# A hybrid encoder layer on one core: the skip product moved into the gate panel, and the first inputs of three stages loaded a stage earlier

## The reference

```python
h = rms_norm(x, norm1_w)
proj = h @ w_in                      # q, k, v, z, xbc, dt_raw, mq
attn_out = windowed_gqa(rope(norm(q)), rope(norm(k)), v, attn_sink)
ssm_out  = ssd_bidirectional(z, xbc, dt_raw, ...)
mem_out  = memory_attention(norm(mq), norm(mk), mv)
x = x + concat([attn_out, ssm_out, mem_out]) @ w_out
return x + (silu(gate) * up) @ w_ffn_down    # gate, up: conv(rms_norm(x) @ w_ffn_up)

# inside ssd_bidirectional
y_f = ssd_scan(xs, dt[0], ...)               # forward scan
y_b = ssd_scan(reversed xs, dt[1], ...)      # backward scan
y = y_f + y_b + d_skip[:, None] * xs         # the skip product
y = rms_norm(y * silu(z)) * norm_w
```

## Time and profile before

| | us |
|---|---|
| median of 3 runs | 2181.43 |
| profiled execution: device time | 2188.39 |
| profiled execution: span | 2186.6 |
| norm and transpose, first load of projections | 0 to 53 |
| `projections` (gate panel from about 449) | 53 to 531.9 |
| `ssm_forward` | 531.9 to 673.9 |
| `attention` | 673.9 to 918.9 |
| `memory` | 918.9 to 1007.4 |
| `out_projection` | 1007.4 to 1246 |
| `ffn` | 1246 to 2186.6 |

### The profile page before, as it was taken

The page is one execution under the profiler, slowest core; times in us unless marked ns, Lnnn a source line. Parts: engine busy times, 40 slices in busy tenths (PEclk is TensorE's granted clock), DMA queues, the critical chain, the costliest instruction groups (busy, mean ns, idle before and its releaser), DMA issues. The chain is left out here.

```text
span 2186.6 us, 29798 instructions
## 1 busy us (share of the span) xinstructions
PE 2034.9 (93%) x10642; PEld 1737.2 (79%) x10642; DVE 1364.8 (62%) x1936; ACT 607.6 (28%) x1172; POOL 233.3 (11%) x242
## 2 busy tenths in 40 slices
PE   4999999997875999788999799999999999999997
PEld 3887888886764999777888588888888888888885
DVE  6664686533873888683324537757766766766766
ACT  5111122112763666541002221211211111121120
POOL 2000584510341001000000000000000000000000
PEclk8999999999776999999999899999999999999998
DMA  5324223223533111244211121111011121010102
GB/s 174 106 87 121 82 102 105 100 93 136 169 125 126 45 39 49 90 162 184 77 39 43 51 72 29 39 48 29 29 58 29 29 58 29 29 58 29 29 10 96
DMA packets 111122, 164.12 MB, mean 75 GB/s; under 512 B 8736, under 2 KB 68160, under 8 KB 109760
## 3 DMA queue, kind: packets, MB, share of 16 engines
q1 hardware_dynamic: 81792, 119.64, 17.2%
q10 hardware_dynamic: 29248, 43.41, 5.6%
HBM read 125.45 MB, written 37.57 MB: 75 GB/s over the span
## 5 line engine op out<-in xcount | busy, mean ns | idle before, releaser
L2373 PE MATMUL ff_proj<-h_hi,ff_uhi 128*128 128x512 f32 (+1 forms) x1056 | 374.8, 355 | 10.7 <-DVE ff_ulo L2286 10.7
L2373 PE MATMUL ff_proj<-h_lo,ff_uhi 128*128 128x512 f32 (+1 forms) x1056 | 374.7, 355 | 0.0
L2373 PE MATMUL ff_proj<-h_hi,ff_ulo 128*128 128x512 f32 (+1 forms) x1056 | 374.4, 355 | 0.0
L2332 DVE TENSOR_TENSOR x<-x,ff_proj 128x512 f32<-128x512 f32 x264 | 181.5, 688 | 185.3 <-PE ff_proj L2393 183.0
L2373 PEld LDWEIGHTS ff_proj<-h_hi,ff_uhi 128*128 128x128 f32 x1056 | 200.3, 190 | 39.9 <-DVE ff_ulo L2286 11.1
L2373 PEld LDWEIGHTS ff_proj<-h_lo,ff_uhi 128*128 128x128 f32 x1056 | 200.3, 190 | 28.6
L2373 PEld LDWEIGHTS ff_proj<-h_hi,ff_ulo 128*128 128x128 f32 x1056 | 200.1, 190 | 28.0
L638 PE MATMUL pj_bank<-pj_whi,act_hi 128*128 128x512 f32 x400 | 160.3, 401 | 0.0
L638 PE MATMUL pj_bank<-pj_whi,act_lo 128*128 128x512 f32 x400 | 156.5, 391 | 0.0
L638 PE MATMUL pj_bank<-pj_wlo,act_hi 128*128 128x512 f32 x400 | 156.5, 391 | 0.0
L2244 ACT ACTIVATE ff_padded<-ff_proj 128x1024 f32<-128x1024 f32 x44 | 45.2, 1028 | 349.4 <-PE ff_proj L2373 349.4
(11 more groups left out here) (269 smaller groups left out, 4205.6 us busy)
## 6 DMA issues: line engine op xcount, KB each, us to landing
ff_rawu<-w_up SPq DMA_DIRECT2D x44, 512.0 KB, 4.8
pj_raw<-w_in SPq DMA_DIRECT2D x28, 512.0 KB, 3.6
ff_rawd<-w_down SPq DMA_DIRECT2D x22, 512.0 KB, 3.5
sf_rows<-scratch_acs_rows SPq DMA_DIRECT2D x10, 1024.0 KB, 7.5
wo_raw<-w_out SPq DMA_DIRECT2D x16, 512.0 KB, 3.6
scratch_proj<-hd_pieces ACTq DMA_DIRECT2D x30, 256.0 KB, 2.1
n_x<-tokens SPq DMA_DIRECT2D x14, 512.0 KB, 4.3
sf_xc<-scratch_xbc_tiles SPq DMA_DIRECT2D x10, 512.0 KB, 4.1
```

The lines of the kernel that those rows point to most:

```text
L2332: nc.vector.tensor_tensor(v, v, ring(g), ALU.add).then_inc(added, 1)
L2373: m = nc.tensor.matmul(proj[:, g, t0:t0 + n], U[w][:, s, k, g], X[x][:, k, t0:t0 + n], start=(k == 0 and r == 0), stop=(k == KC - 1 and r ...
```

## The change

1. The skip product. `scan_back` gets two operations: `y_back = x_ps * D` (read from PSUM, where x has just been turned), then, once y of the state is multiplied into `scaled`, `y_back = y_back + scaled`. `ssm_forward` loses two: the product into `y2` (L1818) and y2 + y_back (L1829); it adds `y_back` itself to y. The wait of ScalarE's B copy for VectorE's y2 goes too.
2. First inputs of the forward scan (identity, norm weights, x, B, C of tiles 0 and 1) are loaded at the end of SyncE's list in `projections`, into free pieces beside `y_back`. The rows and z of tiles 0 and 1 stay where they were.
3. Inputs of `attention` (all keys as one load, the values, queries of tiles 0 and 1, mask, sink, identity) are loaded at the end of SyncE's list in `ssm_forward`.
4. Inputs of `memory` (identity, keys, values, queries of tiles 0 and 1) are loaded at the end of SyncE's list in `attention`.

In each case SyncE waits for these loads before its block ends, and the waits for them in the next stage are gone.

```diff
@@ projections
-        turn_ident = raw[:, 1, 1, 0:P]
+        turn_ident, skip = raw[:, 1, 1, 0:P], raw[:, 1, 1, P:P + NS]
             sp.dma_start(turn_ident, ident_dram).then_inc(S["const"], 16)
+            sp.dma_start(skip, small["ssm_D"].broadcast_to([P, NS])).then_inc(S["const"], 16)
...
                 sp.dma_start(xc[i % 2], xbc_c[NT - 1 - i]).then_inc(xc_loaded[i % 2], 16)
+            sp.wait_ge(head_done, preps)
+            early = ((R["xc"][:, 0], xbc_c[0]), (R["xc"][:, 1], xbc_c[1]), (R["turn_ident"], ident_dram),
+                     (R["norm_w"], small["ssm_norm_w"].broadcast_to([P, NS * PS])))
+            for dst, src in early:
+                sp.dma_start(dst, src).then_inc(forward_loaded, 16)
+            sp.wait_ge(forward_loaded, 16 * len(early))
@@ scan_back
                 v.tensor_tensor(x_dec, x_ps, factor(dec, t), ALU.mult).then_inc(S["x"], 1)
-                dve.wait_ge(S["off"], i + 1)
+                if i == 0:
+                    dve.wait_ge(S["const"], 32)
...
-                v.tensor_tensor(y_back[:, t].rearrange("p (h q) -> p h q", q=PS), y_ps, factor(e_acs, t),
-                                ALU.mult).then_inc(S["y"], 1)
+                v.tensor_tensor(yb, x_ps, bc(skip.unsqueeze(2), [P, NS, PS]), ALU.mult).then_inc(S["x"], 1)
+                dve.wait_ge(S["off"], i + 1)
+                if i > 0:
+                    dve.wait_ge(S["h"], 2 * i)
+                v.tensor_tensor(scaled, y_ps, factor(e_acs, t), ALU.mult).then_inc(S["y"], 1)
+                dve.wait_ge(S["x"], 2 * i + 2)
+                dve.wait_ge(S["y"], 2 * i + 1)
+                v.tensor_tensor(yb, yb, scaled, ALU.add).then_inc(S["y"], 1)
+                dve.wait_ge(S["y"], 2 * i + 2)
                 v.tensor_tensor(scaled, state, factor(e_tot, t), ALU.mult).then_inc(S["h"], 1)
@@ back_inputs, back_states (TensorE)
-                    pe.wait_ge(S["const"], 16)
+                    pe.wait_ge(S["const"], 32)
-                    pe.wait_ge(S["x"], i)
+                    pe.wait_ge(S["x"], 2 * i)
-                pe.wait_ge(S["x"], i + 1)
+                pe.wait_ge(S["x"], 2 * i + 1)
@@ ssm_forward
-            for dst, src in ((ident[:, :], ident_dram), (wn[:, :], small["ssm_norm_w"].broadcast_to([P, XW])),
-                             (dsk[:, :], small["ssm_D"].broadcast_to([P, NS]))):
-                sp.dma_start(dst, src).then_inc(S["const"], 16)
...
             order(sp, load)
+            ahead.load(sp, proj, k_twice, ident_dram, mask_dram, small["attn_sink"], early_loaded)
...
-            pe.wait_ge(S["const"], 48)
...
-                    act.wait_ge(S["y"], 4 * t - 2)
...
-                v.tensor_tensor(hp(y2[:, :]), x_tok[:, :, :], bc(dsk[:, :].unsqueeze(2), [P, NS, PS]),
-                                ALU.mult).then_inc(S["y"], 1)
...
-                v.tensor_tensor(y2[:, :], y2[:, :], yb, ALU.add).then_inc(S["y"], 1)
...
-                v.tensor_tensor(y[:, s], y[:, s], y2[:, :], ALU.add).then_inc(S["y"], 1)
+                v.tensor_tensor(y[:, s], y[:, s], yb, ALU.add).then_inc(S["y"], 1)
@@ attention: its inputs, loaded in ssm_forward
+    def load(self, sp, proj, k_twice, ident_dram, mask_dram, sink, done):
+        for dst, src in ((self.ident[:, :], ident_dram), (self.sink[:, :], sink.broadcast_to([P, HQ])),
+                         (self.k_two[:, :].rearrange("p t h a d -> p t (h a d)"), keys),
+                         (self.q_raw[:, :].rearrange("p t h d -> p t (h d)"), rows[:, 0:2, 0:1024]),
+                         (self.mask[:, :], mask_dram[1]), (self.v[:, :, :], rows[:, :, 1280:1536])):
+            sp.dma_start(dst, src).then_inc(done, 16)
+        sp.wait_ge(done, 16 * self.LOADS)
...
             tile_loop(sp, load)
+            mem_early.load(sp, mem_proj, proj, ident_dram, memory_loaded)
...
-            pe.wait_ge(S["const"], 16 * 2)
             for t in range(NT):
-                pe.wait_ge(k_loaded[sum(t >= t0 for t0, _ in KEY_PARTS[1:])], 16)
@@ memory
-            pe.wait_ge(S["const"], 16)
             for k in range(NMT):
-                pe.wait_ge(k_loaded[k // MT], 16)
```

More of the change, by code:

```diff
@@ L887, in _, with __init__ @@
             act.wait_ge(row_stored, 32 * NCH)
-def attention(nc, proj, k_twice, ident_dram, mask_dram, small, mix_t):
-    sink = small["attn_sink"]
+class AttentionInputs:
+    LOADS = 6
+    def __init__(self, nc, ctx):
+        b = Bufs(nc, ctx)
+        self.ident = b.sb("at_ident", [P, P])
+        self.mask = b.sb("at_mask", [P, 3 * P])
+        self.sink = b.sb("at_sink", [P, HQ])
+        self.k_two = b.sb("at_ktwo", [P, NT, HKV, 2, DH])
+        self.v = b.sb("at_v", [P, NT, HKV * DH])
+        self.q_raw = b.sb("at_qraw", [P, 2, HQ, DH])
+    def load(self, sp, proj, k_twice, ident_dram, mask_dram, sink, done):
+        rows = proj.rearrange("(t p) n -> p t n", p=P)
+        keys = k_twice.rearrange("(t p) n -> p t n", p=P)
+        for dst, src in ((self.ident[:, :], ident_dram), (self.sink[:, :], sink.broadcast_to([P, HQ])),
[4 more added lines that the diff above has]
+        sp.wait_ge(done, 16 * self.LOADS)
@@ new lines, with __init__, far, load @@
+class MemoryInputs:
+    LOADS = 4
+    def __init__(self, nc, ctx):
+        def far(name, shape):
+            return ctx.enter_context(nc.sbuf_tensor(name, shape, FP32, side="right"))
+        self.ident = far("me_ident", [P, P])
+        self.k_n = far("me_kn", [P, NMT, HM, DM])
+        self.v = far("me_v", [P, NMT, HM, DM])
+        self.q_n = far("me_qn", [P, 2, HM, DM])
+    def load(self, sp, mem_proj, proj, ident_dram, done):
+        kv = mem_proj.rearrange("(t p) n -> p t n", p=P)
+        queries = proj.rearrange("(t p) n -> p t n", p=P)
+        for dst, src in ((self.ident[:, :], ident_dram),
+                         (self.k_n[:, :].rearrange("p t h d -> p t (h d)"), kv[:, :, 0:512]),
+                         (self.q_n[:, :].rearrange("p t h d -> p t (h d)"), queries[:, 0:2, 2048:2560]),
+                         (self.v[:, :].rearrange("p t h d -> p t (h d)"), kv[:, :, 512:1024])):
+            sp.dma_start(dst, src).then_inc(done, 16)
+        sp.wait_ge(done, 16 * self.LOADS)
@@ L901, in attention @@
+def attention(nc, proj, early, mem_proj, mem_early, ident_dram, mix_t):
     WIN = 3 * P
-    KEY_PARTS = ((0, 2), (2, 4), (6, NT - 6))
     with ExitStack() as ctx:
         b = Bufs(nc, ctx)
-        ident = b.sb("at_ident", [P, P])
-        mask = b.sb("at_mask", [P, WIN])
-        k_two = b.sb("at_ktwo", [P, NT, HKV, 2, DH])
-        v_sb = b.sb("at_v", [P, NT, HKV * DH])
+        ident, mask, k_two, v_sb, sinkb, q_raw = early.ident, early.mask, early.k_two, early.v, early.sink, early.q_raw
@@ L1012, in high @@
         def high(act, t, s):
-            act.wait_ge(q_loaded[s], q_loaded_value(t, s))
+            if not (isinstance(t, int) and t < 2):
+                act.wait_ge(q_loaded[s], q_loaded_value(t, s))
             if not (isinstance(t, int) and t == 0):
@@ L1225, in _, with memory @@
                 o_unit(NT - 1, c, units_before(NT - 1) + 3 + c)
-def memory(nc, proj, mem_proj, ident_dram, mix_t, w_out, first):
+def memory(nc, proj, early, mix_t, w_out, first):
     MT = NMT // 2
@@ L1514, in _, with ssm_forward @@
             o_t(NT - 1)
[L1517 removed]
+def ssm_forward(nc, proj, xbc_c, acs_rows, ident_dram, small, R, mix_t, k_twice, mask_dram, ahead):
     XW = NS * PS
@@ L1640, in body @@
                 first = before(t, 1)
-                pe.wait_ge(loaded[s], loaded_value(t, s))
+                if not before(t, 2):
+                    pe.wait_ge(loaded[s], loaded_value(t, s) - 16)
                 if not first:
```

96 lines of the change are left out of this document (33 added, 63 removed).

## The result

The changed kernel takes 2165.24 us, the median of 4 runs (2158.49 to 2167.82), beside 2184.47 us for 4 runs of the kernel before (2181.31 to 2187.79). The ratio is 0.991 (0.9894 to 0.9927): 19.2 us by the medians. A second set of 5 runs gave 2163.05 us and 0.9885 (0.9864 to 0.9906). The profiled execution has a span of 2164.3 us and a time of 2166.04; the sum had put them at 2164.4 and 2166.2. So the size is right in total, and two of the sum's four terms, looked at one by one, are not: the starts of the scan and of the memory stage.

The account below looks back on a forecast made before the run. The prediction took the kernel to be bound by serial stages whose starts wait for loads. Gains of 2.9 (scan), 13.9 (attention), 5.4 (memory) and 0 (skip product) sum to 22.2 us: from 2181.43 to 2159.2 us, range 2149 to 2171.

Parts of the forecast that it names:

- the sum's four terms: Gains at the starts of scan, attention and memory plus the skip product: 2.9 + 13.9 + 5.4 + 0 = 22.2 us.
- Bound by serial starts: Seven blocks run without overlap, so time at a block's start in which nothing computes is kernel time.
- Start of the scan: Forward scan: TensorE starts at once, but the rows are late next, landing in 5.95 us; gain 2.9 us.
- my signs of being wrong: Scan products with other than five 6.9 us runs; VectorE's last panel wait gone; a block's end following a load.
- Start of attention: Attention: TensorE starts at about 673.96 instead of 687.87, the chain of keys keeping its pace; gain 13.9 us.
- Start of the memory stage: Memory stage: TensorE no longer waits for the identity; gain 5.4 us, lower end 1.9.
- rival of the clock: Scan: the alternation of fast and slow tiles shifts; 16.3 us either way; better by over 6 us 0.09, worse 0.10.
- Skip product, 0: Scan: two VectorE operations fewer per tile, hidden by other waits; gain 0, upper end 3.3 us.
- Panel: Gate panel: VectorE's two added operations, 1.4 us per tile, fit its 2.34 us wait; cost 0. Slower rival: 0.02.
- early loads: End of the scan: attention's 5128 KB of loads end some 10 us before the block does and cost nothing.
- spill: End of the scan: rival that prefetch at half rate ends the block 7.5 us later, gain 14.7; chance 0.04.
- all fast: Scan: the clock rival's better case, all ten tiles' products fast, 16.3 us more gain, 2142.9 us.

Follow-up runs that it names:

- e2: The changed kernel with the memory stage's first inputs loaded inside the memory stage again; 2169.86 us, ratio 0.9922.
- e3: The changed kernel with attention's first inputs loaded inside attention again; 2177.77 us, ratio 0.9961.
- e4: The changed kernel with the scan's identity, norm weights and first x, B, C loaded inside the scan again; 2169.67 us, ratio 0.9926.
- f0: The changed kernel run once more, nothing altered; 2163.05 us.
- g3: The kernel before the change with the same unread matmuls at the same places as g1; 2170.22 us, ratio 0.9926.
- g1: The changed kernel with unread matmuls in TensorE's idle stretches in the scan, attention and the memory stage's end; 2142.27 us, ratio 0.9797.
- e1: The kernel before with only the skip product moved to the gate panel; 2185.78 us, ratio 1.0005.
- f1: The changed kernel with three unread matmuls of 384 columns at the end of TensorE's list in attention; 2160.59 us, ratio 0.9897.
- f2: The changed kernel with 28 unread matmuls where TensorE waits in the forward scan; 2149.16 us, ratio 0.9838.
- f3: The changed kernel with the scan's first tile's rows loaded as two transfers; 2160.43 us, ratio 0.9891.
- h1: g1 with the skip product made in the forward scan again, as before the change; 2143.54 us, ratio 0.9810.
- g2: g1 with the first tile's rows also loaded in two transfers; 2145.09 us, ratio 0.9813.

## Why the prediction was right, and where it was not

**Bound by serial starts.** Right. Each of e2, e3 and e4 lengthens its own stage, and by the medians their parts, 21.6 us, are as large as the whole change (19.2 and 21.9).

**Start of the scan, 2.9 us.** The step was right and its size was not: 4.3. I took the rows' landing as 5.95 us, the middle of a load that was alone (5.1) and one in a row of others (6.8); it was 4.6, and 4.5 to 5.0 in the other profiles. The scan gained 5.8 in the profile and 5.1 against e4. What goes beyond 4.3 lies in the tail: from the second product to the last 95.06 us instead of 96.00, and 0.6 us less behind it, with products of 5.81 and 6.43 us where before stood 3.68 and 7.06. That is how the clock fell in this run, the rival that I had named, at a tenth of its price; in f0, the same kernel, the stretch from the second product to the last took 93.67. So one of my signs of being wrong did come: not five slow products but six, three of them at 6.9 us or more and three between the levels.

**Start of attention, 13.9 us.** Right: 13.9 for e3 against after and 13.6 for before against f0, each pair with the same kind of first tile, and 13.7 for g3 against g1. The chain of keys kept its pace too, as I had said: from TensorE's start to the turn of the queries it took 8.42 us, and 8.76 before. That the profiled stage gained only 12.1 is the clock, at 0.51 from 677 to 687 over the first tile's scores. It was low there in e1 and e3 as well, where the loads are late, and not in f0: chance between runs, which the sum had at nothing in this stage.

**Start of the memory stage, 5.4 us.** Wrong in size: 2.8. The step that failed is taking the whole wait as gain. The wait of 5.4 us went, and 2.6 came back, since TensorE came to the first tile at the lower level and stayed there for 12.5 us instead of 3.0. f1 shows that it is the clock: at 0.99 the stage takes 79.48 us, which is 9.0 less than before. I had asked of each start what would be late next among buffers and transfers, and not at what clock the freed engine would work; my rival of the clock was for the scan alone. f0, e3 and e4 repeat it (12 us at the lower level). f2 and f3, with 3 to 4 us of it, show that it doesn't have to be so, and what decides stays open.

**Skip product, 0.** Right: e1 holds 0. h1 adds that the move shows 1.5 to 1.8 us when the slow products are gone; that these hide it otherwise is argued and not shown.

**Panel, early loads, spill.** Right. VectorE's last wait fell by 1.25 us and the tiles kept their 7.9; the loads were down 8 us before the end (I had said some 10).

**The sum.** 22.2 us against 22.3 of the two profiled spans is partly luck: +1.4 from the scan, +1.5 from its tail, +1.4 from chance ahead of it, -1.8 (attention) and -2.6 (memory) from the clock. Against the medians, 19.2 and 21.9, it is 3.0 and 0.3 us high. The forecast of 2159.2 stood 6.0 under the median after, since I took the gain from the median of three runs; over 23 runs the kernel before took 2185.55.

**The rival of the clock** came nearest to mattering. I had priced "all fast" at 16.3 us and given it to chance. It can be brought about: f2 has nine of ten products fast and its scan is 12.0 us shorter. The Trainium skill, "TensorE: Matmul & The Clock Gate", section "HAM oscillation", says that waits between bursts of matmuls throw the clock back each time. The traces agree with it in part: with the waits filled nine of ten products are fast (f2), but unfilled only every second one was slow before, not each.

## What to carry to other kernels

Where stages don't overlap, the time from a stage's first issue to its first work can be summed over the stages, and loads a stage earlier take it away where all the inputs move; here they landed 8 us before that stage's end and cost it nothing. In the scan, where the rows stayed, only 4.3 of the 9.0 us before ScalarE's first work on them went. But ask of each freed start at what clock TensorE will come to it: read the granted clock by 4 us before and after the start. Where its level changes with every tile, some matmuls into a free bank, put where TensorE waits anyway, can be worth as much as the change itself (28 of them made the scan 12 us shorter here, beside some 20 us for all the early loads). And before a difference between two profiled stages is put down to the change, look whether the clock fell in the same places in both.

## What the runs showed of the hardware

- The level in a stage's first microseconds is not a property of the kernel: attention's first scores took 0.58 us in one run of the changed kernel and 0.38 in the next, and the same fillers at attention's end stand ahead of a memory stage at 1.00 in f1 and of one that falls to 0.50 within 2 us in g1, g2 and h1. What decides between them stays open; no run here shows it.
- A filler costs little: three matmuls of 128x384 took 2.10 us in f1, in 3.7 us without other work.
- A load of 1 MB to 128 partitions, the first of its stage, landed in 4.5 to 5.0 us (eight profiles). In halves, the first landed in 4.2 and 4.1 us and the second in 5.1 and 5.3 (f3, g2).
